# The last attention pass of a diffusion layer: the output's squares, mean, normalising scale and low part take other places in the queues of ScalarE, VectorE and TensorE

## The reference

```python
def diff_attn_block(q, k, v, lam):
    s = jnp.einsum('bqhnd,bkhnd->bnhqk', q, k).astype(jnp.float32) * (1.0 / math.sqrt(HEAD_DIM))
    a = jax.nn.softmax(s, axis=-1)
    a = a[:, 0] - lam * a[:, 1]
    return jnp.einsum('bhqk,bkhv->bqhv', a.astype(v.dtype), v)
...
    attn = (rms_norm(attn, subln_g) * (1.0 - lam_i)).reshape(B, T, ATTN_WIDTH)
```

## Time and profile before

| | |
|---|---|
| median of 3 runs (lowest to highest) | 3197.71 us (3194.93 to 3198.88) |
| the profiled execution, its span | 3195.74 us, 3194.0 us |
| busy share of the span: PE, PEld, DVE, ACT, POOL | 97%, 88%, 70%, 51%, 22% |
| the last pass, steps 2 to 14, from the first exponential of step 2 to that of step 15 | 1505.64 to 1667.29 us, 13 steps |
| granted clock over the whole execution | 0.988 |

### The profile page before, as it was taken

How to read it: one execution, slowest core, us unless ns; L and a number is a source line. 1 busy time by engine, 2 the same in 40 slices (tenths; PEclk the granted TensorE clock), 3 DMA queues, 4 the chain that set the end, 5 groups by cost and what they waited for, 6 DMA issues and landing times. The chain is left out here.

```text
span 3194.0 us, 67304 instructions
## 1 busy us (share of the span) xinstructions
PE 3092.1 (97%) x22490; PEld 2802.7 (88%) x22490; DVE 2229.7 (70%) x3915; ACT 1623.1 (51%) x3603; POOL 697.6 (22%) x902
## 2 busy tenths in 40 slices
PE   7989999999999999998999997999999999999999
PEld 5989989998998998997887776999999999998998
DVE  5888878888887887887884557555555555555554
ACT  4656666666666665665872225333433333333332
POOL 2532233333333333332210002111111111111111
PEclk9999999999999999999999997999999999999999
DMA  8754444345335345344335556666555555555664
GB/s 292 260 196 123 127 131 144 116 120 156 120 115 156 121 125 157 120 128 139 117 120 193 199 183 201 196 196 199 186 185 185 185 185 185 185 185 185 197 200 132
DMA packets 341256, 530.38 MB, mean 166 GB/s; under 512 B 29690, under 2 KB 256250, under 8 KB 325882
## 3 DMA queue, kind: packets, MB, share of 16 engines
q1 hardware_dynamic: 330956, 493.47, 47.0%
q0 software_dynamic: 10160, 35.13, 4.4%
HBM read 439.10 MB, written 88.64 MB: 165 GB/s over the span
## 5 line engine op out<-in xcount | busy, mean ns | idle before, releaser
L3201 PE MATMUL ps_gu<-xT,e_w 128*128 128x272 f32 x6144 | 775.9, 288 | 1.1 <-DVE xT L3399 1.1
L3201 PEld LDWEIGHTS ps_gu<-xT,e_w 128*128 128x128 f32 x6144 | 772.1, 188 | 2.5 <-issue 1.3
L1228 ACT ACTIVATE e<-ps_s,negm 128x1024 f32<-128x1024 f32 (+2 forms) x416 | 474.0, 1144 | 238.9 <-DVE negm L1658 200.8
L1643 DVE TENSOR_REDUCE mx<-ps_s 128x1 f32<-128x1024 f32 (+3 forms) x428 | 525.6, 1234 | 68.3 <-PE ps_s L849 67.4
L849 PE MATMUL ps_s<-kT,qT 128*128 128x512 f32 (+1 forms) x1920 | 479.3, 387 | 14.0 <-ACT e L1228 12.9
L3388 DVE TENSOR_TENSOR e_w<-e_raw,e_w 128x2048 fp32r<-128x2048 f32 x126 | 288.5, 2290 | 207.6 <-ACT e_w L3259 207.6
L849 PEld LDWEIGHTS ps_s<-kT,qT 128*128 128x128 f32 x1920 | 341.0, 190 | 92.5 <-ACT e L1228 33.7
L926 PE MATMUL ps_m<-w,hT 128*128 128x384 f32 x2040 | 391.0, 339 | 3.9 <-DVE o L1710 3.9
L891 PE MATMUL ps_m<-v,aT 128*128 128x128 f32 x2816 | 367.5, 277 | 1.5 <-ACT aT L1212 1.5
L926 PEld LDWEIGHTS ps_m<-w,hT 128*128 128x128 f32 x2040 | 348.3, 188 | 5.4 <-issue 5.4
L891 PEld LDWEIGHTS ps_m<-v,aT 128*128 128x128 f32 x2816 | 337.5, 191 | 5.7 <-ACT aT L1212 3.3
(11 more groups left out here) (442 smaller groups left out, 4199.1 us busy)
## 6 DMA issues: line engine op xcount, KB each, us to landing
hT<-hT_d SPq DMA_DIRECT2D x85, 1024.0 KB, 5.3
e_raw<-w_gate SPq DMA_DIRECT2D x48, 1024.0 KB, 5.2
e_raw<-w_up SPq DMA_DIRECT2D x48, 1024.0 KB, 7.5
e_raw<-w_down SPq DMA_DIRECT2D x32, 1024.0 KB, 14.8
e_raw_more<-w_down SPq DMA_DIRECT2D x32, 1024.0 KB, 7.9
tab<-tabs_d SPq DMA_DIRECT2D x85, 256.0 KB, 2.7
hT_d<-hT SPq DMA_DIRECT2D x17, 1024.0 KB, 3.9
w_lent<-w_ada SPq DMA_DIRECT2D x16, 1024.0 KB, 5.6
```

Of the source, the lines that this page charges most:

```text
L1228: nc.scalar.activation(out, src, ACT.Exp, bias=negm[:, s.par, c:c + 1], scale=HD ** -0.5, accum_out=acc).then_inc(exp_done.sem, 1)
L1643: nc.vector.tensor_reduce(mx[:, c, n:n + 1], ps_s[:, at:at + hi - lo], AX, ALU.max).then_inc(mx_part.sem, 1)
L3201: mm = nc.tensor.matmul(ps_gu[:, 2 * (s % 2) + f, 0:SLOTS], w_view(s, a)[:, k, f * P:f * P + P], xT[:, b, k, :], start=(k == 0 and a + b = ...
```

## The change

Nothing is computed otherwise; instructions change places in three queues, and three waits are added and one removed.

- ACT: in a sample's step `square_out` goes from behind `evacuate` to behind `copy_turned` 1. `normal_out` goes from ahead of `copy_turned` 2 to between the first two exponentials of the second map. The wait for `o_lo` ahead of the third exponential of the second map is gone.
- DVE: `mean_square` goes from behind the second mix to behind the second map's `fold`. `low_out` leaves the end of the step; it stands in the next step, behind the first maximum of the first map.
- PE: the third group of the first map's scores waits for `low_out` (its bank holds the turned output), and so does `turn_out`.
- The prompt's step: PE turns and multiplies the fourth lot (`turn` 4, `weighted` 3) ahead of the scores, and DVE does `low_out` of two steps, one ahead of the maximum and one at the end.

```diff
@@ -816,6 +816,8 @@
 
                     if n == 2 and c == 1:
                         mod2_done.wait(pe, s, 1)
+                    if n == 2 and c == 0 and s.front == "sample" and late(previous(s)):
+                        o_lo.wait(pe, previous(s))
                     if c == 1 and s.front == "sample":
                         exp_done.wait(pe, s, n + 1)
                     elif s.front == "sample" and not s.zero:
@@ -1092,12 +1094,16 @@
             def late_body(s):
 
                 p = previous(s)
+                if s.front != "sample":
+                    turn(p, 4)
+                    weighted(p, 3)
                 scores(s, 0, slice(0, 1))
-                if late(p):
+                if late(p) and s.front == "sample":
                     turn(p, 4)
                 scores(s, 0, slice(1, None))
                 if late(p):
-                    weighted(p, 3)
+                    if s.front == "sample":
+                        weighted(p, 3)
                     weighted(p, 4)
                 if s.j is not None or s.i < NS:
                     modulation_half(s)
@@ -1111,6 +1117,7 @@
                 weighted(s, 2)
                 if late(p):
                     mx_part.wait(pe, s, 2 * maxima_of(s))
+                    o_lo.wait(pe, p)
                     turn_out(p)
                 turn(s, 3)
 
@@ -1219,8 +1226,6 @@
                 for n, (lo, hi) in list(enumerate(groups_of(s)))[some]:
                     if n == 2 and c == 0:
                         ada2_done.wait(act, s, 1)
-                    if n == 2 and c == 1 and late(previous(s)):
-                        o_lo.wait(act, s)
                     if s.front == "sample":
                         out, src, acc = e[:, s.par, c, lo:hi], ps_s[:, lo:hi], l3[:, s.par, c, n:n + 1]
                     else:
@@ -1406,16 +1411,20 @@
                 exps(s, 0, slice(0, 1))
                 if late(p):
                     evacuate(p)
+                if s.front != "sample":
                     square_out(p)
                 exps(s, 0, slice(1, None))
                 if s.j is not None or s.i < NS:
                     keep_half(s)
                 copy_turned(s, 0)
                 copy_turned(s, 1)
+                if late(p) and s.front == "sample":
+                    square_out(p)
+                copy_turned(s, 2)
+                exps(s, 1, slice(0, 1))
                 if late(p):
                     normal_out(p)
-                copy_turned(s, 2)
-                exps(s, 1, slice(0, 2))
+                exps(s, 1, slice(1, 2))
                 if late(p):
                     high_out(p)
                 copy_turned(s, 3)
@@ -1915,8 +1924,14 @@
                     coefficient(s)
                     mix(s, 0)
                     mix(s, 1)
+                if s.front != "sample":
+                    exp_done.wait(dve, s)
+                    low_out(previous(p))
                 for n in range(len(groups_of(s))):
                     maximum(s, 0, n)
+                    if n == 0 and s.front == "sample" and late(p) and late(previous(p)):
+                        exp_done.wait(dve, s)
+                        low_out(previous(p))
                     if n == 1:
                         fold(s, 0)
                 negate(s, 0)
@@ -1924,17 +1939,20 @@
                     coefficient(s)
                     mix(s, 0)
                     mix(s, 1)
+                if s.front != "sample":
                     mean_square(p)
                 mix(s, 2)
                 for n in range(len(groups_of(s))):
                     maximum(s, 1, n)
                     if n == 1:
                         fold(s, 1)
+                        if late(p):
+                            mean_square(p)
                 negate(s, 1)
                 mix(s, 3)
                 mix(s, 4)
                 first_sums(s)
-                if late(p):
+                if s.front != "sample":
                     low_out(p)
                 if s.j is None and s.i == NS:
                     add_bias(s)
```

## The result

The changed kernel takes 3204.29 us (median of 10 runs, 3202.91 to 3207.83) against 3197.61 us before (10 runs, 3192.85 to 3200.90). The ratio is 1.0024, with a 95% interval of 1.0016 to 1.0031: 5.1 to 9.9 us slower. The forecast was 3208 us in a range of 3197 to 3214, and slower with 0.82. The profiled execution of the changed kernel has a span of 3201.2 us (3194.0 before).

The account below looks back on a forecast made before the run. Neither DVE nor PE is full; a loop of hand-overs bounds steps 2 to 14. Second halves +11.3, first halves -1.0 and prompt's step +0.1 give +10.4 us on the 3197.71 median: 3208 us, range 3197 to 3214.

Parts of the forecast that it names:

- The term that decides: Second half of steps 2 to 14: `normal_out` late delays `turn_out` and next scores; +0.87 us a step (0.73 to 1.00).
- `low_out` between the maxima: DVE, next step's start: its 0.27 us stays inside the chain to the bias, ahead of the first maximum or the second.
- The first half: First exponential of first map to that of second, steps 2 to 15: -0.07 us a step (gain 0.23 to none).
- The added waits: Third group's wait for `low_out`: PE's idle time just covers it; at worst up to 0.1 us lost a step.
- The prompt's step: Prompt's step, PE's scores and the mean's wait for squares: +0.1 us in all, bounds -0.5 and +0.7.
- The sum: Steps' second halves +11.3, first halves -1.0, prompt's step +0.1: together +10.4 us, bounds +5.8 and +15.1.
- nothing behind the barrier can hide the difference: The change ends before a barrier, so later stages cannot hide the difference; no size given.
- a time that moves in the stages behind: Sign of being wrong: time moving in stages behind the pass, which the change doesn't touch; no size given.
- One sign: Sign of being right: a step's first maximum waits about 0.8 us for PE's scores, formerly for the high part.
- The first (the waits go and nothing takes their place): Steps 2 to 14: 12.0 us of waits vanish on DVE, the busier engine; 3186 us; chance 5%.
- The second (PE's wait hidden): `turn_out` holds nothing up; only the first half's gain, 1 to 3 us, is left: 3194 to 3197; chance 12%.
- The third: PE's added idle time lowers the clock in the pass: up to 20 us more, 3220 and over; chance 3%.

Follow-up runs that it names:

- Experiment three: Kernel before, with `normal_out` alone moved on ScalarE between the second map's two wide exponentials: ratio 1.0032 to the kernel before, 3206.62 us.
- experiment one: Changed kernel, with `turn_out` moved behind the next step's first scores on TensorE alone: ratio 1.0004 to the kernel before, 3198.15 us.
- the fourth experiment: Changed kernel, with one more activation, a copy that nothing reads, ahead of `normal_out` in the samples' steps: 3207.88 us in a single run.
- experiment two: Kernel before, with `low_out` and its waits alone moved between the next step's first two maxima: ratio 1.0003 to the kernel before, 3197.65 us.
- experiment five: Kernel before, with `turn` 4 and `weighted` 3 ahead of the scores in the prompt's step on TensorE alone: 3194.64 us in a single run.
- experiment six: Changed kernel, with the prompt's step in the old order on TensorE, scores before the fourth lot: 3206.91 us in a single run.
- experiment seven: Changed kernel, with `normal_out` early again, squares behind the second exponential, mean at DVE's wait for PE: ratio 0.9990 to the kernel before, 3192.73 us.

## Why the prediction was right, point by point

- *The term that decides* held: the second half of a step grew by 0.83 us (0.87 forecast, bounds 0.73 and 1.00). Its parts: `turn_out` loaded at E + 1.68 (1.60), since 0.18 and not 0.10 lie between ACT's end and PE's load; but the turn and the scores follow faster, at E + 2.19 (2.20); first maximum E + 3.42 (3.46); next A E + 6.90 (6.94). Experiment three makes this loss with that move alone, one takes it away without touching the move, and four shows that what is added ahead of `normal_out` comes out at the step's end undiminished.
- *`low_out` between the maxima* costs what it gave, 0.27 inside the chain either way: experiment two, a gain of 0.04 a step.
- *The first half* gained 0.10 (0.07 forecast), limited by PE's own queue as it said: the wait of 0.18 at the second group is gone and the maximum comes 0.16 earlier.
- *The added waits* cost little in the changed kernel, inside the bound of 0.1: the modulation's loads (1676.52 to 1677.46 in step 15, so to E + 8.11) end just ahead of the second map's scores, which are loaded at A + 1.31 in place of A + 1.25. (The terms that the prediction names for that end add up to E + 8.10, not to its 8.17.) With the scores early again (experiment one) DVE's new wait is the last to end, 0.23 a step: its cover was the delay itself.
- *The prompt's step* came to -0.07 (+0.1 forecast, bounds -0.5 and +0.7), but of two parts that I had not priced apart: the order on TensorE gains 0.5 (experiment five), what moved on the other engines takes it back. With the old order the changed kernel's stretch was 1.7 us longer, at a lower clock (experiment six, one trace).
- *The sum* of +10.4 us was 9.5 in the part that it prices (9.57 and -0.07) and +6.7 in the medians. 9.5 lies inside the interval of 5.1 to 9.9, but the two profiled executions as wholes differ by 7.2 only. So the sentence that nothing behind the barrier can hide the difference did not hold for them, and one of the prediction's own signs of being wrong, a time that moves in the stages behind, did show: -1.69 us, of which 1.51 is the clock in one place of the output stage. Over the nine traces the start of step 2 lies between 1505.0 and 1507.4 us and the part behind the pass's stretch is 1494.5 to 1496.6 us long, without regard to what was changed, so single executions differ by some 2 us each there. Whether the other runs of the two kernels differ in that clock too, and so whether it makes the medians' 6.7, is open.
- *One sign was sized wrong.* The first maximum waits 1.62 us for scores, not about 0.8. The sum itself says so: by the earlier trace rows DVE is free at E + 1.80 (1663.81 less its wait of 0.79), and E + 3.46 less that is 1.66.
- *The rivals.* The first (the waits go and nothing takes their place) fell: DVE's waits for the high part and the squares did go, 12.0 us, and its waits for scores grew by 16.7. That DVE is the busier engine holds against TensorE's weight loads (140.12 and 136.67 us in the earlier trace rows); against its matmuls as recorded, with ends that the profile models, 157.34, it does not. The rule of the Trainium skill, Perfetto Trace Analysis, section Identifying the Most-Contended Engine, to optimize first the engine with the highest occupancy, did not show the way here: DVE lost 12.0 us of its waits and the steps took 9.57 us longer, since DVE waited on another engine's queue. The second (PE's wait hidden) fell by the 1.11 us ahead of `turn_out`. The third fell for the pass, at a granted clock of 1.00 with that wait in each step.

## What to carry to other kernels

An instruction that is off the critical path has a place in a queue, and what stands behind it may be on the path: before it is made later, look who waits for it, and what stands behind that waiter. Here the normalised output was nobody's hurry, but TensorE's transpose of it stood in front of the next step's scores. The repair is either end of the hand-over: move the waiter behind the urgent work (experiment one), or place the producer in a gap of its own engine that lies early enough (experiment seven, a mean in front of a wait and a normalisation in ScalarE's idle time). A wait that such a move removes is worth only the time to the next wait behind it: here 0.79 us went, and the first maximum came 0.31 earlier (experiment two).

## What the runs showed of the hardware that was not expected

- The granted clock fell from 1.00 (2.4 GHz, the upper level) to 0.50 (1.2 GHz, the lower) for some 3 us in the prompt's step of three kernels, after waits of PE of 1.5, 1.7 and 2.3 us, and not in the kernel before, after 2.4 us of the same kind, nor in the pass, where PE's matmuls stood idle for 0.95 us in each step. In all five traces that have eight products in the gap it stayed at 1.00. In the output stage it fell after an idle time of 3.27 us in one trace and not after 3.28 in another. What sets the fall off in one case and not in the other stays open. It cost 1.5 to 1.6 us in the prompt's step (4.00 to 4.03 us in place of 2.46) and 1.5 in the output stage.
- Two activations of 128 columns on ScalarE start 0.19 or 0.20 us apart in all 14 steps of the fourth experiment, though they are recorded with 0.30 and 0.39.
